# A hybrid decoder layer on one core: turning the attention probabilities with transposing DMAs, and a new slot table beside the MLP

## The chip, the cores and the metric

The kernel runs on one core of one Trainium2 chip, in one launch. The metric is the device time of that core in microseconds, lower is better. The number before the change is the median of three runs.

## The reference

One inference step of one layer for a prompt of 2048 tokens (width 1024) and 32 sampled tokens. What matters here is the banded attention (A with window 128 and sinks; C with three dilations 1, 4, 16) that is computed beside the matrix products of the layer:

```python
def hybrid_layer(h, W, l, past):
    u = rmsnorm(h, W['norm_mix_g'][l])
    proj = u @ W['w_in'][l]                      # qa ka va qc kc vc z xbc dt
...
    oa, _ = banded_attention(qa, ka, va, WIN_A, 1, tab_a, W['a_sinks'][l])
    for window, dil in C_BRANCHES:               # (128,1), (512,4), (2048,16)
        o, s = dilated_banded_attention(qc, kc, vc, window, dil, tab_c)
...
    y, h_last = ssd_chunked(xs, dt, A, bm, cm, h0)   # the scan, chunks of 128
    h = h + mixed @ W['w_out'][l]
    u2 = rmsnorm(h, W['norm_mlp_g'][l])
    h = h + jnp.square(jax.nn.relu(u2 @ W['w_up'][l])) @ W['w_down'][l]

# inside banded_attention, per block of 128 queries and its 256 keys
    logits = jnp.einsum('nbqhgd,nbshd->nbhgqs', qb, kb) + bias
    probs, lse = softmax_with_sink(logits, valid[None, :, None, None], sk)
    out = jnp.einsum('nbhgqs,nbshd->nbqhgd', probs, vb)
```

## The kernel before

The program has three parts: `tokens` and `settle` (input projection, up to about 299 us) and `core`. In `core` the 2048 + 32 tokens go in four blocks (`PIECES`, 512 tokens each, the last 512 + 32). First comes a part called the columns (`col`, to about 717 us). Then comes the trunk: for each block the output projection (`out`), its norm, and four quarters of the MLP, each eight `up` and eight `down` units. A dense unit is 24 matmuls of 128x128 by 512 columns: each product is taken three times on f16 halves (high x high, high x low, low x high).

`plan()` writes the order of all units, and every engine walks the same list. The last 16 dense units of a block host nothing, so 56 slots remain, one behind each of the others. In these slots the block b hosts the small work of block b+1, with b = 0, 1, 2 (called the first, second and third host below). The words for it are:

- a tile of attention: 128 queries by 256 keys, 4 heads. The trunk has 18 tiles in each host, 12 of them real (the others only load keys and values for their neighbour); all 36 real tiles have a previous block. `att` slot k of before does three things at once: the values of tile k-3 (`give_values`, L2573, the product with V), the turning of tile k-2 (`turn_p`, L2588: eight f32 transposes of 128x128 by TensorE into banks 3 and 4, from where ScalarE L1884 and VectorE L2142 write the high half `p_hi` and the low half `p_lo`), and the scores of tile k-1 (`score`, L2603; VectorE L2123 adds the bias and takes the top, ScalarE L1891 the exponential).
- `scan`: three parts of one chunk of the scan; part 1 keeps VectorE from L2251 to L2267. `weigh`/`turn` join the branches.
- `sk`, `sv` (L2727) with `split` (ScalarE L1975, VectorE L2385): the attention of the sampled tokens, in the second and third host.
- in the first host the weights of the MLP come raw (`core_staged`, 512 KB for a dense unit), are split by ScalarE L1794 and VectorE L2043, and are stored for the other blocks.

All DMAs of `core` are issued by SyncE (SP) in the order of the units. SP waits in order: behind a wait stand the weight loads of later units (`fetch`, four slots ahead), the loads for tiles (`load_qkv`, a transposing DMA L1450 of up to 256 KB from DRAM and a plain one L1455), and the store of a tile's output (`store_o`, L1462, waits for VectorE L2107). PSUM has two banks for dense units and six spare ones; `claim()` lets a unit wait until the last user of its bank is through.

## Time and profile before

| | us |
|---|---|
| median of 3 runs (2426.82 to 2431.17) | 2430.77 |
| the profiled execution, whole | 2431.39 |
| its span, first to last instruction | 2429.5 |
| TensorE busy | 2333.6 (96%) |
| VectorE busy | 1193.9 (49%) |
| ScalarE busy | 839.9 (35%) |
| GpSimd busy | 299.5 (12%) |
| mean TensorE clock granted | 0.988 |

TensorE is busy nearly all the time, the others half of it or less. Shares are averages: in the hosting slots VectorE, SP and the DMA engines have much more to do than in the last block. A transposing DMA stands in the trace as an instruction of SP's queue with the time that SP was held by it, and with the time from issue to landing.

### The profile page before, as it was taken

Reading aid. Unit: us, or ns where it says so; the run is one execution under the profiler, and the core shown is the slowest. Engines: PE = TensorE matmul, PEld = TensorE weight load, DVE = VectorE, ACT = ScalarE, POOL = GpSimd, SP = SyncE. Lnnn points to the kernel's source line nnn. Section 1 sums busy time; section 2 is a strip of 40 time slices with the busy share of each in tenths; the row PEclk is TensorE's granted clock in tenths of the full one; section 3 lists DMA queues with packets and bytes.
Section 4 is the critical chain, followed back from the end, with each engine's and each line's share of the span. In section 5 each row is a group of like instructions: output and inputs, shape, how many; then the busy total and the mean of one; then the engine's idle time right before and its main releaser. Section 6 shows DMA issues by size and latency. Waiting matters only on the chain. (4 is left out here: it accounts for less than half of the span.)

```text
span 2429.5 us, 42324 instructions
## 1 busy us (share of the span) xinstructions
PE 2333.6 (96%) x17134; PEld 1355.8 (56%) x17134; DVE 1193.9 (49%) x2680; ACT 839.9 (35%) x1580; POOL 299.5 (12%) x316
## 2 busy tenths in 40 slices
PE   6999889999899999999999999999999999999999
PEld 3555445555345555444555554445555456888887
DVE  5676475565647666633655562155555522321222
ACT  5454354555445445322433321034334112210110
POOL 1122223102012211001111200101111001000000
PEclk9999999999999999999999999999999999999999
DMA  7746587775558877875665565445554553222222
GB/s 253 257 165 222 177 224 197 213 223 169 174 192 224 213 212 238 260 250 158 154 159 162 167 190 171 139 132 127 151 182 157 173 159 114 89 95 96 96 96 85
DMA packets 396759, 419.94 MB, mean 173 GB/s; under 512 B 130453, under 2 KB 325525, under 8 KB 396310
## 3 DMA queue, kind: packets, MB, share of 16 engines
q1 hardware_dynamic: 396276, 416.79, 56.9%
q8 instruction: 137, 2.24, 0.4%
q14 instruction: 56, 0.46, 0.1%
q10 hardware_dynamic: 290, 0.45, 0.1%
HBM read 280.31 MB, written 118.96 MB: 164 GB/s over the span
## 5 line engine op out<-in xcount | busy, mean ns | idle before, releaser
L2478 PE MATMUL core_dense<-core_u,tok_ring 128*128 128x512 f16 (+2 forms) x4800 | 863.6, 340 | 7.8 <-DVE core_u L2063 7.5
L2478 PEld LDWEIGHTS core_dense<-core_u,tok_ring 128*128 128x128 f16 x4800 | 465.9, 98 | 377.5 <-DVE core_u L2063 11.4
L2478 PE MATMUL core_dense<-core_r_hi,tok_ring 128*128 128x512 f16 (+2 forms) x2560 | 651.4, 340 | 1.7 <-DVE core_r_lo L2082 1.7
L2478 PE MATMUL core_dense<-core_r_lo,tok_ring 128*128 128x512 f16 (+2 forms) x1280 | 434.7, 340 | 0.0
L2478 PEld LDWEIGHTS core_dense<-core_r_hi,tok_ring 128*128 128x128 f16 x2560 | 250.6, 98 | 197.5 <-DVE core_r_lo L2082 2.7
L2478 PE MATMUL core_dense<-tok_u,tok_ring 128*128 128x512 f16 x1104 | 256.0, 388 | 10.8 <-PEq L866 8.1
L1861 ACT ACTIVATE core_r<-core_dense 128x512 f32<-128x512 f32 (+2 forms) x160 | 82.3, 515 | 470.0 <-PE core_dense L2478 469.8
L2079 DVE TENSOR_TENSOR core_r<-core_r 128x512 f32<-128x512 f32 (+2 forms) x160 | 96.7, 604 | 290.0 <-ACT core_r L1861 289.6
L766 PE MATMUL tok_prod<-tok_w_hi,tok_u 128*128 128x512 f16 (+1 forms) x768 | 198.1, 347 | 3.5 <-DVE tok_u L622 3.5
L2478 PEld LDWEIGHTS core_dense<-tok_u,tok_ring 128*128 128x128 f16 x1104 | 106.8, 100 | 140.7 <-issue 19.7
L2478 PEld LDWEIGHTS core_dense<-core_r_lo,tok_ring 128*128 128x128 f16 x1280 | 125.4, 98 | 94.5 <-issue 1.5
L1891 ACT ACTIVATE core_p<-core_p,core_neg 128x256 f32<-128x256 f32 (+1 forms) x256 | 99.7, 460 | 184.6 <-DVE core_neg L2130 184.5
L2091 DVE SCALAR_TENSOR_TENSOR core_h<-core_dense,core_h 128x512 f32<-128x512 f32 (+1 forms) x96 | 58.3, 607 | 211.8 <-PE core_dense L2478 211.7
L766 PE MATMUL tok_prod<-tok_w_lo,tok_u 128*128 128x512 f16 (+1 forms) x384 | 133.2, 347 | 0.0
L2043 DVE SCALAR_TENSOR_TENSOR tok_ring<-core_staged,tok_ring 128x1024 f16<-128x1024 f32 x72 | 88.9, 1235 | 71.3 <-ACT tok_ring L1794 69.9
L1733 POOL TENSOR_TENSOR core_v_hi<-core_v_raw,core_ones 128x256 f16<-128x256 f32 (+1 forms) x82 | 62.1, 758 | 490.1 <-DMA core_v_raw<-out_tok 338.0
L766 PEld LDWEIGHTS tok_prod<-tok_w_hi,tok_u 128*128 128x128 f16 x768 | 74.6, 98 | 65.8 <-DVE tok_u L622 6.6
L2190 DVE SCALAR_TENSOR_TENSOR core_col<-core_conv_raw,core_cw,core_col 128x512 f32<-128x512 f32 x96 | 76.1, 793 | 63.0 <-ACT core_conv_raw L1815 60.8
L2082 DVE TENSOR_TENSOR core_r_lo<-core_r,core_r_hi 128x512 f16<-128x512 f32 (+2 forms) x160 | 97.2, 608 | 17.0 <-DVE core_r L2079 0.5
L2091 DVE SCALAR_TENSOR_TENSOR core_h_more<-core_dense,core_h_more 128x512 f32<-128x512 f32 (+1 forms) x64 | 36.2, 565 | 131.6 <-PE core_dense L2478 131.6
L1771 POOL TENSOR_TENSOR core_ssum<-core_ssum,core_r 128x512 f32<-128x512 f32 (+1 forms) x24 | 30.9, 1286 | 564.8 <-ACT core_r L1840 564.8
L2123 DVE CUSTOM_DVE_ANT_0 core_p<-core_spare,core_bias 128x256 f32<-128x256 f32 (+1 forms) x256 | 81.4, 373 | 23.7 <-PE core_spare L2603 18.2
(327 smaller groups left out, 2564.2 us busy)
## 6 DMA issues: line engine op xcount, KB each, us to landing
tok_ring<-scratch_kept_w SPq DMA_DIRECT2D x262, 512.0 KB, 4.4
scratch_kept_w<-tok_ring SPq DMA_DIRECT2D x72, 512.0 KB, 5.5
core_staged<-in_w_up SPq DMA_DIRECT2D x32, 512.0 KB, 4.6
core_staged<-in_w_down SPq DMA_DIRECT2D x32, 512.0 KB, 4.2
out_tok<-tok_tok SPq DMA_DIRECT2D x16, 644.0 KB, 3.1
core_piece<-in_c_kt SPq DMA_DIRECT2D x32, 288.0 KB, 3.9
core_piece<-in_c_v SPq DMA_DIRECT2D x16, 576.0 KB, 4.5
scratch_sums<-core_o SPq DMA_DIRECT2D x64, 132.0 KB, 3.6
```

What stands on the lines that cost most here:

```text
L766: last = pe.matmul(bank[0:nt, 0:w], l, r[:, k, c0:c0 + w], start=k == 0 and i == 0, stop=k == KT - 1 and i == 2, skip_group_check=True)
L1733: pool.tensor_tensor(hi, v, ones[:, 0:w].rearrange("p (h d) -> p h d", d=HD), ALU.mult).then_inc(vh_ready, 1)
L1771: pool.tensor_tensor(ssum[:, 0:w], ssum[:, 0:w], r[:, i % 2, 0:w], ALU.add).then_inc(summed, 1)
L1861: act.activation(r[:, n % 2, 0:w], bank_of["up", b, f, q][:, 0:w], ACT.Relu, scale=1.0 / (WS * HS)).then_inc(r_ready, 1)
L1891: last = act.activation(p[:, hh, cols], p[:, hh, cols], ACT.Exp, bias=neg[:, hh:hh + 1])
L2043: dve.scalar_tensor_tensor(ring[:, q % R, :, 1, :], w_raw[n % RW], WS, ring[:, q % R, :, 0, :], ALU.mult, ALU.subtract).then_inc(lo_split, 1)
L2079: dve.tensor_tensor(r2[:, n % 2, 0:w], r[:, n % 2, 0:w], r[:, n % 2, 0:w], ALU.mult).then_inc(r2_ready, 1)
L2082: dve.tensor_tensor(r_lo[:, f % HF, off:off + w], r2[:, n % 2, 0:w], r_hi[:, f % HF, off:off + w], ALU.subtract).then_inc(rl_ready, 1)
L2091: dve.scalar_tensor_tensor(here, bank_of["down", b, i, q][:, 0:w], HS * HS / WS, here, ALU.mult, ALU.add).then_inc(down_added, 1)
L2123: last = dve.tensor_tensor_reduce(p[:, hh, cols], spare[1 + bank][:, :].rearrange("p (a c) -> p a c", c=2 * P)[:, at, cols], bias[:, BIAS_ ...
L2190: dve.scalar_tensor_tensor(dst, conv_raw[:, i, j:j + 512], cw[:, i, j:j + 1], dst, ALU.mult, ALU.add).then_inc(tap, 1)
L2478: ins = pe.matmul(bank, w[:, k, part, :], s, start=first and j == 0, stop=last and j == 2, skip_group_check=True)
```

## The change

For the 36 tiles of the trunk (`by_dma`) TensorE turns nothing. ScalarE (`high`) and VectorE (`low`) write the two f16 halves of the probabilities from SBUF into `p_half`, 128 x 1024 each, and SP issues two transposing DMAs of 256 KB from SBUF to SBUF (`turn_p`, into `p_t`). The four steps of a tile are units of their own: S scores and softmax, one slot later H the halves, one slot later T the DMAs, two slots later O the values. A new tile begins every second slot. The three parts of a scan chunk now stand two slots apart in the odd slots, among the tiles, ten slots from chunk to chunk; before, they stood behind the last tile. The joins follow as before. Banks: O has bank 4, B of the scan bank 3 and CB bank 5 (chunks from 4 on), `sk` always banks 3 and 0. The bias table has two buffers in place of three, so that it is loaded again for each run of tiles of a kind. The 28 tiles before the trunk keep the old way.

```diff
-bias = a.sb("bias", [P, 3, 4, 2 * P])
+bias = a.sb("bias", [P, 2, 4, 2 * P])
...
-p_hi = a.sb("p_hi", [P, 8, P], F16)
-p_lo = a.sb("p_lo", [P, 8, P], F16)
+p_t = a.sb("p_t", [P, 2, 8, P], F16)
+p_hi, p_lo = (p_t[:, i, :, :] for i in range(2))
+p_half = a.sb("p_half", [P, 2, 8, P], F16)
+half_ready, pt_in = a.sems("half_ready", 2), a.sems("pt_in", 2)
...
+reals = [[n for n in range(first, end) if att[n][3]] for first, end in zip([0] + att_end[:-1], att_end)]
+bias_runs = [(kind, [n for n, _ in run]) for kind, run in itertools.groupby(
+    ((n, att[n][0]) for group in reals for n in group), key=lambda tile: tile[1])]
+run_of = {n: r for r, (_, run) in enumerate(bias_runs) for n in run}
+def by_dma(n):
+    return n >= att_end[1]
+def dma_no(n):
+    return real_no[n] - real_no[att_end[1]]
+HOST_FROM = (2, 2, 4)
...
-            some = [[] for _ in range(HOST_FROM[b])] + [[s] for s in att_slots(att_end[b + 1], att_end[b + 2])]
-            for c in range(4 * b + 4, 4 * b + 8):
-                x1, x2, x3 = scan_parts(c)
-                some += [[x1], [], [x2], [x3]]
+            some = [[] for _ in range(56)]
+            for m, n in enumerate(reals[b + 2]):
+                at = HOST_FROM[b] + 2 * m
+                some[at].append(("S", n, 0, 0))
+                some[at + 1].append(("H", n, 0, 0))
+                some[at + 2].append(("T", n, 0, 0))
+                some[at + 4].append(("O", n, 0, 0))
+            some[at + 6].append(("sums", 4 * b + 4, 0, 0))
+            for c in range(4):
+                for part, unit in zip((0, 2, 4), scan_parts(4 * b + 4 + c)):
+                    some[HOST_FROM[b] + 1 + 10 * c + part].append(unit)
             j = joins(b + 1)
-            some += [[j[0]], [], [j[1], j[2]], [], [j[3], j[4]], [], [j[5], j[6]], [], [j[7]]]
-            some += [[]] * (56 - len(some))
+            for k, those in enumerate(([j[0]], [j[1], j[2]], [j[3], j[4]], [j[5], j[6]], [j[7]])):
+                some[HOST_FROM[b] + 38 + 2 * k] += those
...
+SK_BANKS = (3, 0)
+def b_bank(c):
+    return 1 if c < 4 else 3
+def cb_bank(c):
+    return 2 if c < 4 else 5
+def o_bank(n):
+    return 4 if by_dma(n) else 5
...
+        def load_bias(r):
+            kind, run = bias_runs[r]
+            if r >= 2:
+                sp.wait_ge(top, real_no[bias_runs[r - 1][1][0]])
+            sp.dma_start(bias[:, r % 2, :, :], lines_at(io, kind, P - 1, [[LINE - 1, P], [P * LINE, 4], [1, 2 * P]])).then_inc(bias_in[r % 2], 16)
+        def turn_p(n):
+            e = real_no[n]
+            sp.wait_ge(o_done, e)
+            for i in range(2):
+                sp.wait_ge(half_ready[i], dma_no(n) + 1)
+                sp.dma_start_transpose(p_t[:, i, :, :], p_half[:, i, :, :].rearrange("p a c -> p (a c)")).then_inc(pt_in[i], 16)
...
+            scored = b if kind == "S" else k - 1 if kind == "att" and b <= k - 1 < i else None
+            r = run_of.get(scored, 0)
+            if r and scored == bias_runs[r][1][0] and r + 1 < len(bias_runs):
+                load_bias(r + 1)
+            if kind == "S":
+                while next_qkv < min(b + 4, len(att)):
+                    load_qkv(next_qkv)
+                    next_qkv += 1
+            elif kind == "T":
+                turn_p(b)
+            elif kind == "sums":
+                load_sums(b)
...
+        def soften(n):
+            act.wait_ge(neg_ready, real_no[n] + 1)
+            for hh in range(4):
+                last = act.activation(p[:, hh, :], p[:, hh, :], ACT.Exp, bias=neg[:, hh:hh + 1])
+            last.then_inc(p_ready, 1)
+        def high(n):
+            act.wait_ge(p_ready, real_no[n] + 1)
+            if dma_no(n):
+                act.wait_ge(pt_in[0], 16 * dma_no(n))
+            act.activation(p_half[:, 0, :, :].rearrange("p a c -> p (a c)"), p[:, :, :].rearrange("p h c -> p (h c)"), ACT.Copy).then_inc(half_ready[0], 1)
...
+        def keep_values(n):
+            e = real_no[n]
+            dve.wait_ge(o_done, e + 1)
...
+        def score(n):
+            kind, _, _, _, prev = att[n]
+            e, r = real_no[n], run_of[n]
+            cols = slice(0, 2 * P) if prev else slice(P, 2 * P)
+            if kind == 0:
+                dve.wait_ge(const_in, 64)
+            dve.wait_ge(bias_in[r % 2], 16 * (r // 2 + 1))
+            dve.wait_ge(s_done, e + 1)
...
+            if by_dma(n) and dma_no(n):
+                dve.wait_ge(half_ready[1], dma_no(n))
...
+        def low(n):
+            dve.wait_ge(half_ready[0], dma_no(n) + 1)
+            if dma_no(n):
+                dve.wait_ge(pt_in[1], 16 * dma_no(n))
+            flat = [t.rearrange("p a c -> p (a c)") for t in (p_half[:, 1, :, :], p[:, :, :], p_half[:, 0, :, :])]
+            dve.tensor_tensor(*flat, ALU.subtract).then_inc(half_ready[1], 1)
...
-            pe.wait_ge(lo_ready, 2 * e + 2)
+            if by_dma(n):
+                for i in range(2):
+                    pe.wait_ge(pt_in[i], 16 * (dma_no(n) + 1))
+            else:
+                pe.wait_ge(lo_ready, 2 * e + 2)
...
-                last = pe.transpose(spare[1][:, gr * P:(gr + 1) * P], xbc[:, c % 2, 4 + gr, :], ident[:, :])
+                last = pe.transpose(spare[b_bank(c)][:, gr * P:(gr + 1) * P], xbc[:, c % 2, 4 + gr, :], ident[:, :])
```

What stands on SP's queue in the first host, before. L1385 loads raw weights, L1392 stores split ones, L1450 and L1455 load a tile, L1462 stores an output:

```order
L1385 DMA core_staged<-in_w_up 128x8x128
L1392 DMA scratch_kept_w<-tok_ring 128x2048
L1450 DMA_TRANSPOSE core_qk_t<-scratch_tok_h 128x4x128
L1455 DMA core_v_raw<-out_tok 128x256
L1462 DMA scratch_sums<-core_o 128x264
L1385 DMA core_staged<-in_w_up 128x8x128
L1392 DMA scratch_kept_w<-tok_ring 128x2048
L1450 DMA_TRANSPOSE core_qk_t<-scratch_tok_h 128x8x128
L1455 DMA core_v_raw<-out_tok 128x256
```

And in the changed kernel, in the same host (L1417 raw weights, L1424 the store, L1502 the output, L1482 the new DMAs, L1490 and L1495 a tile):

```order
L1417 DMA core_staged<-in_w_down 128x8x128
L1424 DMA scratch_kept_w<-tok_ring 128x2048
L1417 DMA core_staged<-in_w_down 128x8x128
L1424 DMA scratch_kept_w<-tok_ring 128x2048
L1502 DMA scratch_sums<-core_o 128x264
L1482 DMA_TRANSPOSE core_p_t<-core_p_half 128x8x128 x2
L1490 DMA_TRANSPOSE core_qk_t<-scratch_tok_h 128x8x128
L1495 DMA core_v_raw<-out_tok 128x256
L1490 DMA_TRANSPOSE core_qk_t<-scratch_tok_h 128x2x128
L1495 DMA core_v_raw<-out_tok 128x128
```

The two new DMAs stand behind the store of the output of the tile before, and in front of the loads for later tiles.

TensorE in the third host, before: the scores of a tile, a dense unit, the turning of that tile, the products of a sampled piece (L2727), a dense unit.

```order
L2603 MATMUL core_spare<-core_qk_t 128x128 x24
L2478 MATMUL core_dense<-core_u,tok_ring 128x512 x24
L2588 MATMUL core_spare<-core_ident,core_p 128x128 x8
L2727 MATMUL core_spare<-core_pt,core_halves 128x16 x3
L2727 MATMUL core_spare<-core_pt,core_halves 128x8 x3
L2727 MATMUL core_spare<-core_pt,core_halves 128x2 x24
L2478 MATMUL core_dense<-core_u,tok_ring 128x512 x24
```

And changed:

```order
L2699 MATMUL core_spare<-core_qk_t 128x128 x24
L2570 MATMUL core_dense<-core_u,tok_ring 128x512 x24
L2823 MATMUL core_spare<-core_pt,core_halves 128x16 x3
L2823 MATMUL core_spare<-core_pt,core_halves 128x8 x3
L2823 MATMUL core_spare<-core_pt,core_halves 128x2 x24
L2570 MATMUL core_dense<-core_u,tok_ring 128x512 x24
```

The eight transposes between the dense unit and the sampled products are gone; nothing stands in their place.

## Rows read from the trace of the kernel before

**Rows 1.** TensorE's waits from 717 us on: total us, times, longest.

```profile
PE core_spare L2727 <- DVE core_halves L2385: 5.0, 5, 1.6
PE core_spare L2727 <- DVE core_y L2273: 2.9, 4, 1.2
PE core_dense L2478 <- DVE core_r_lo L2082: 1.7, 2, 1.2
...
PE core_spare L2727 <- DVE core_o L2107: 0.2, 1, 0.2
```

**Rows 2.** Timeline of TensorE, first host: start us, us, line, operation.

```profile
789.13 0.19 PE L2573 MATMUL core_spare<-core_v_hi,core_p_hi 128*128 128x65 f16 x1
...
789.86 1.07 PE L2588 MATMUL core_spare<-core_ident,core_p 128*128 128x128 f32 x8
790.86 0.84 PE L2603 MATMUL core_spare<-core_qk_t 64*128 64x128 f16 x24
791.64 0.39 PE L2478 MATMUL core_dense<-core_r_hi,tok_ring 128*128 128x512 f16 x1
```

**Rows 3.** L2588 in windows: PE busy (x), PEld busy (x), clock, DMA share, GB/s.

```profile
1100.00:1500.00 400.00, 12.79 (x96) 10.54 (x96) 1.00 0.58 164
```

**Rows 4.** Transposing DMAs from DRAM, 717 to 1800 us: SP held (ns), and landing.

```profile
L1450 SPq DMA_TRANSPOSE core_qk_t<-scratch_tok_h x51: 1188/1599/2477, 735.8 to 1737.2; - x51
...
DMA to landing us min/median/max: 3.8/5.6/7.3
```

**Rows 5.** DMA issues: count, KB each, median us from issue to landing.

```profile
out_y<-core_yt SPq DMA_DIRECT2D x32, 256.0 KB, 2.4
...
core_h<-scratch_xt SPq DMA_DIRECT2D x16, 256.0 KB, 4.4
```

**Rows 6.** Timeline of all engines in the third host, behind an `up` unit.

```profile
1726.34 0.19 PE L2573 MATMUL core_spare<-core_v_hi,core_p_hi 128*128 128x65 f16 x1
...
1727.16 0.84 PE L2603 MATMUL core_spare<-core_qk_t 64*128 64x128 f16 x24
...
1727.93 5.35 PE L2478 MATMUL core_dense<-core_u,tok_ring 128*128 128x512 f16 x24
...
1729.36 0.15 DVE L2107 COPY core_o<-core_spare 128x4 f32<-128x4 f32 x1
...
1730.92 0.17 DVE L2130 TENSOR_SCALAR core_neg<-core_o 128x4 f32<-128x4 f32 x1
...
1733.12 1.04 PE L2588 MATMUL core_spare<-core_ident,core_p 128*128 128x128 f32 x8
...
1733.92 1.36 DVE L2385 TENSOR_TENSOR core_halves<-core_piece,core_halves 128x1152 f16<-128x1152 f32 x1 [2.83 <-ACT core_halves L1975]
...
1735.34 0.81 PE L2727 MATMUL core_spare<-core_pt,core_halves 128*128 128x8 f16 x25 [1.18 <-DVE core_halves L2385]
```

**Rows 7.** Timeline behind a `down` unit, second host.

```profile
1246.71 0.19 PE L2573 MATMUL core_spare<-core_v_hi,core_p_hi 128*128 128x65 f16 x1
...
1247.97 0.15 DVE L2107 COPY core_o<-core_spare 128x4 f32<-128x4 f32 x1
```

**Rows 8.** Timeline of VectorE in part 1 of a scan chunk, first host.

```profile
870.85 0.68 DVE L2251 TENSOR_TENSOR core_xdt<-core_spare,core_small 128x512 f32<-128x512 f32 x1
...
872.05 0.41 DVE L2255 TENSOR_TENSOR core_cb_low<-core_spare,core_upper 128x256 f32<-128x256 f32 x1
...
877.52 0.68 DVE L2267 TENSOR_TENSOR core_state<-core_state,core_small 128x512 f32<-128x512 f32 x1
```

**Rows 9.** Timeline of TensorE in part 2 of a chunk, third host.

```profile
1788.95 0.44 PE L2708 MATMUL core_spare<-core_dec,core_xdt 128*64 128x128 f32 x4
...
1790.85 1.13 PE L2716 MATMUL core_spare<-core_xte,core_b_tok 128*128 128x256 f32 x4
```

**Rows 10.** Window, first host: PE, PEld, DVE, ACT, POOL busy (x), clock, DMA share, GB/s.

```profile
735.00:855.00 120.00, 119.42 (x1062) 66.86 (x1061) 79.06 (x201) 58.18 (x104) 24.60 (x30) 1.00 0.88 222
```

**Rows 11.** VectorE, groups from 717 to 1160 us: busy us, mean ns, idle before.

```profile
L2043 DVE SCALAR_TENSOR_TENSOR tok_ring<-core_staged,tok_ring 128x1024 f16<-128x1024 f32 x62 | 76.0, 1226 | 46.2 <-ACT tok_ring L1794 44.8
```

114 lines of the change are left out of this document (60 added, 54 removed).

## The prediction

> **What bounds the kernel.** I read the table first: TensorE is busy for 96% of the span. Then its waits from 717 us on, where the change lies: they are few, and those that the change can touch are 5.0 + 2.9 + 0.2 us before the sampled products (L2727) and 1.7 us at the start of a quarter's `down` units [rows 1]. So what leaves TensorE there leaves the time, as long as nothing new makes it wait. The timelines then show how much slack each neighbour has; "u" below is the moment at which TensorE begins a tile's values behind a dense unit, and all offsets count from it.
>
> **Part 1, the transposes leave TensorE.** In [rows 2] the eight transposes begin at 789.86 and the scores behind them at 790.86: 1.00 us for a tile. As busy time it is 12.79 us for twelve tiles, 1.07 each [rows 3]. 36 tiles: **-36 us** (ends -35 and -38). Scores, values and dense units keep their count.
>
> **Part 2, the way by DMA, and what the steps wait for.** In [rows 6] scores follow u by 0.82 (1727.16), the dense unit by 1.59 (1727.93), and it ends at +6.78 (1733.12), so it takes 5.19. In the changed order the next values stand two dense units later: 1.59 + 2 x 5.19 = **+11.97** is TensorE's own pace for a tile. The DMAs of that next tile stand on SP behind the store of this tile's output, and that waits for VectorE's copy, which ends at +3.17 behind an `up` unit (1729.51) [rows 6] and at +1.41 behind a `down` unit (1248.12 against 1246.71) [rows 7]. With some 0.35 for the store the first transposing DMA can start at +3.5 or +1.8. About half of the 36 are of each kind.
>
> How long both take is the unknown. Transposing DMAs from DRAM hold SP for 1.19 to 2.48 us, median 1.60, and land 3.8 to 7.3 after issue, median 5.6 [rows 4]; no row has one from SBUF. Two in a row: at least 1.2 + 3.8 = 5.0, at the medians 1.6 + 5.6 = 7.2, at most 2.5 + 7.3 = 9.8. Plain DMAs of 256 KB land in 2.4 us from SBUF and 4.4 from DRAM [rows 5], two us apart; I take half of that off the median: **6.2 us** for the pair. Then the values find their data at +9.7 behind `up`, +8.0 behind `down`, before +11.97, and TensorE would not wait.
>
> But there is a second loop. VectorE's `low` of a tile waits for the landing of the tile before (its buffer is single), VectorE is in order, and behind `low` stand the raw split of the first host (1.23 us) [rows 11], the `up` work (1.4) and the copy (0.5) that releases the next DMAs. Its length is 6.2 + low 1.3 + split 1.2 + up 1.4 + copy and store 0.9 = **11.0 us in the first host**, against 11.97; 9.8 in the other two. It fits by a little, until a scan chunk comes in: part 1 keeps VectorE from 870.85 to 878.20, 7.35 us [rows 8], parts 2 and 3 some 4 more with their waits on ScalarE, and TensorE gets only about 4.7 us of scan work for all three (3.0 for part 2, from 1788.95 to 1791.98) [rows 9]. Before, the chunks stood behind the tiles and this did no harm. Now three of four chunks of a host are among the tiles: +11.3 - 4.7 = 6.6 us for a chunk, less 5 tiles x 1.0 of slack in the first host, leaves some 2 us a chunk. That is 3 x 2 at the values behind the chunks, and 2 more at the first `down` units, which need the last `up` unit's low half from a late VectorE: **+8 us**. In the second host the slack of 5 x 2.2 covers the chunk; sampled products now share banks 3 and 0 with the scan, and at two slots TensorE waits some 1.5 for a copy, of which 0.9 to 1.3 each is no new kind: **+2**.
>
> The transfers: the first host already has a DMA share of 0.88 at 222 GB/s [rows 10]. 24 transfers of 256 KB are 6.3 MB more in some 175 us, 36 GB/s or 0.14 of share, about what the longer stretch for the same tiles gives back. So I add nothing, but the landing may rise here; that is in the range.
>
> **Part 3, the sampled products of the third host.** TensorE can take a piece only when VectorE has its low half. Behind `up` this is at +8.94 (1735.28) [rows 6], since the scores' softmax goes first, and TensorE came there at +7.78, after the turning of the tile: it waited 1.18. With no turning it comes at +6.78 and waits 2.2. Part of what Part 1 takes off is given back here. Over the eight pieces that stand behind a slot with scores: two beside no scan behind `up` 2.2 each, one with part 3 of the scan 1.3, one behind `down` 0.9 (there VectorE is some 1.3 earlier), together 6.6. Where part 1 of a scan stands in the slot the piece also waits for bank 5, which CB now has: L2251 to L2255 are 1.6 us [rows 8] behind `low`, so 3.3 twice, and 2.5 once behind the tiles. Part 2 of the scan has bank 5 as well, as before, but its y is now behind `low`: 2.5 and 0.8. Sum 19.0 against 8.1 before [rows 1]: **+11 us**.
>
> **Part 4, small things.** The 1.7 us at the `down` units go in their old places (their price in the new ones is in Part 2): **-1.7**. ScalarE and VectorE make the halves from SBUF instead of PSUM, 1024 columns each, no more than now. SP also passes T's waits with its weight loads behind it; those are four slots ahead, some 21 us, and SP comes free at about +10, so nothing. The bias is loaded seven times more, a run of four tiles ahead: nothing.
>
> **Sum.** 2431.4 (the profiled execution) - 36 + 8 + 2 + 11 - 1.7 = 2414.7. That execution is 0.6 above the median of the runs: **2415** after rounding up.
>
> **The rivals.** What moves the sum is the time of the DMA pair. From 6.2 to 7.4 the same walk gives 18 in the first host, 3 in the second and 14 in the third: 14 us more for 1.2 us.
>
> - *Quick landing.* The pair takes 5.0, the least that rows 4 allow: first host +3, second +1, third +8: 2431.4 - 36 + 12 - 1.7 = 2406, and 2396 if the bank waits are hidden as well. For it: SBUF as the source [rows 5]. Against it: SP was held longer in the busy first host. The Trainium skill (Advanced Engine Details and Errata, X-Bar Transpose) says that transposing DMAs on TRN2 are as fast as regular ones; rows 4 and 5 show 5.6 against 4.4 us from DRAM, so the trace does not bear it out in full, and by that rule the sum would be this rival's.
> - *Landing as from DRAM, or in a crowd.* 7.2 to 7.4 a pair: 2431.4 - 36 + 18 + 3 + 14 - 1.7 = 2429, the gain eaten; with a bit more crowding 2436.
> - *SP held per block of the source, slower than before.* If the source in SBUF makes SP issue longer, 2.5 us each, and the second lands at 7.3, the pair takes 9.8. Then the data come at +13.3 behind `up` (late by 1.4), and VectorE's loop is 14.6 in the first host and 13.4 in the others against 11.97: about 1.8 for each of 36 tiles, 66 us in place of the 10 of Part 2: 2431.4 - 36 + 66 + 14 - 1.7 = 2474. The sum passes 2431 where the pair takes some 7.6 us, and grows then by 12 or more for each us. For it: every tile pays, nothing overlaps within a pair. Against it: no row above 2.5. Where it takes 8.4, it is some 2442.
> - *Blocks one by one.* A pair has 16 blocks of 128x128. The Trainium skill (VectorE: DVE Perf Modes, The three transpose paths) gives 1309 ns for one by DMA against 390 on TensorE, and advises TensorE where PSUM will do. Eight blocks landed in 5.6 us in rows 4, not in 10.5, so the trace speaks against the sum of singles; if it held, the pair would be 21 us, the loop 27, and 36 x 14 us would make it about 2900.
>
> **How the numbers follow.** Forecast (2406 to 2424) 0.42. Quick landing, below 2406, 0.10. As from DRAM (2424 to 2437) 0.22, of which 0.03 below 2426, 0.15 within 0.2% of 2430.8 (2425.9 to 2435.6) and 0.04 above. SP held longer 0.24, blocks one by one 0.02. So faster by over 0.2% 0.55, within 0.2% 0.15, slower 0.30; 0.2% is about what a measurement of this kernel can tell from no change. The range goes from 2397 (all waits of Part 3 hidden) to 2460, which leaves out 0.03 below and about 0.14 above. The likeliest case has 2406 to 2424 of its own.
>
> **What would show it.** No L2588 row for the trunk and TensorE's busy time down by 36 to 38 us (Part 1). The new DMAs' hold and landing: a median hold of 1.6 and landing of 4.6 is the forecast; 2.5 or more is the slower rival. TensorE's waits at the values (L2573's successor) put down to the landing of `p_t` or to VectorE, some 8 to 10 us, nearly all in the first host; waits at L2727's successor near 19 us in the third host. If those at the values are above 40 us, Part 2 is wrong; if those at the sampled products are 8 us or less, Part 3 is.

## The result, and the profile after

| | median us | range | ratio to before, 95% interval |
|---|---|---|---|
| kernel before | 2428.8 | 2423.98 to 2431.17 | |
| changed kernel | 2471.6 | 2468.61 to 2473.75 | 1.0176, 1.0161 to 1.0191 |

The change makes the kernel 1.8% slower; 2415 was forecast, in a range up to 2460. The page of the changed kernel, first its table of engines: busy us, share of the span, instructions.

```profile
span 2468.0 us, 41862 instructions
...
PE 2327.9 (94%) x16846; PEld 1333.7 (54%) x16846; DVE 1191.8 (48%) x2644; ACT 836.9 (34%) x1544; POOL 306.9 (12%) x316
```

Against 2429.5 and 2333.6 before, TensorE's idle time grew from 95.9 to 140.1 us (+44.2), and its busy time fell by 5.7 us only, though 36 transposes of a tile had left it (38.1 us as busy time). To see where, cut the trace at the same four places of the program: the start of the trunk, and the last transposes of y (L2551 before, L2643 after) in each of the first three blocks. The stretches in between are the first, second and third host, and a last block that hosts nothing. Of each: start:end, length, PE busy, PEld, DVE, ACT, POOL busy, the granted clock, DMA share, GB/s. The kernel before:

```profile
717.00:1150.00 433.00, 430.18 (x2644) 218.37 (x2645) 252.30 (x487) 170.62 (x283) 57.63 (x58) 1.00 0.73 217
1150.00:1597.00 447.00, 444.71 (x3610) 229.91 (x3607) 206.59 (x493) 129.98 (x239) 52.58 (x58) 1.00 0.56 161
1597.00:2057.00 460.00, 451.64 (x3339) 251.22 (x3339) 216.54 (x527) 134.47 (x259) 48.74 (x52) 0.99 0.51 151
2057.00:2429.00 372.00, 362.51 (x3116) 304.59 (x3116) 97.90 (x212) 60.25 (x140) 0.00 (x0) 1.00 0.29 94
```

and the changed one:

```profile
715.00:1170.00 455.00, 429.31 (x2544) 211.84 (x2545) 251.50 (x474) 169.78 (x271) 57.33 (x58) 0.97 0.77 222
1170.00:1622.00 452.00, 440.14 (x3515) 222.67 (x3515) 205.72 (x482) 129.03 (x227) 56.97 (x58) 0.98 0.65 176
1622.00:2096.00 474.00, 451.58 (x3246) 244.09 (x3247) 214.91 (x515) 133.28 (x247) 51.45 (x52) 0.97 0.56 162
2096.00:2468.00 372.00, 362.23 (x3116) 304.28 (x3114) 97.40 (x211) 60.16 (x140) 0.00 (x0) 1.00 0.29 94
```

The exact lengths are 432.6, 447.4, 460.2 before and 454.9, 452.1, 473.6 after. The last block is the same to 0.1 us, so the loss is in the hosts. Length less PE busy is TensorE's idle time: 2.8, 2.3 and 8.4 us before, 25.7, 11.9 and 22.4 after. The column behind POOL is the second part of the loss: the granted clock, 1.00, 1.00 and 0.99 before, is 0.97, 0.98 and 0.97. The trace's record of the clock adds up, in the three hosts, to 3.4, 0 and 6.8 us at the half level (1.2 GHz) before, and to 27.2, 13.6 and 30.6 after (whole records; the one at the start of the first host lies over its edge, 0.7 us before and 2.3 after). Half of that time is lost. This closes the account of each host; the price paid is the measured growth plus the 12 us that the transposes had taken:

| | idle | clock | 12 tiles not turned | sum | measured | price forecast | price paid |
|---|---|---|---|---|---|---|---|
| first | +22.9 | +11.9 | -12 | +22.8 | +22.4 | +8 | 34.4 |
| second | +9.6 | +6.8 | -12 | +4.4 | +4.6 | +2 | 16.6 |
| third | +14.0 | +11.9 | -12 | +13.9 | +13.4 | +11 | 25.4 |

One number of this table leans on its execution. In the traces of two experiments below that leave the third host of the kernel before as it was, this host took 455.9 and 456.5 us, not 460.2, and had no time at the half level. Against those the third host grew by 17 us, and the account closes as well (clock +15.3). The other two are steady: 432.3 and 433.9, and 447.2.

The waits themselves, TensorE's from 717 us on (what waited and for what: us in total, times, longest), which answer to [rows 1]:

```profile
PE core_spare L2669 <- DMA core_p_t<-core_p_half: 15.1, 8, 3.7
PE core_spare L2823 <- DVE core_cb_low L2341: 9.6, 3, 3.7
PE core_spare L2823 <- DVE core_halves L2471: 8.5, 5, 2.3
PE core_spare L2818 <- DVE core_dt_all L2477: 4.7, 1, 4.7
PE core_dense L2570 <- DVE core_r_lo L2154: 4.5, 1, 4.5
PE core_spare L2812 <- DVE core_dt_all L2477: 4.4, 1, 4.4
PE core_spare L2823 <- DVE core_y L2359: 3.8, 3, 2.6
...
PE core_spare L2699 <- issue: 2.6, 1, 2.6
PE core_spare L2804 <- issue: 2.3, 2, 1.5
PE core_spare L2782 <- DVE core_dt_all L2477: 1.7, 1, 1.7
```

L2669 are the values, all eight waits in the first host; L2823 are the sampled products, L2812, L2818 and L2782 parts of the scan that wait for a bank. "issue" means that the trace shows nothing that was waited for. And how the clock looks on the way: three stretches of 20 us in the third host of the changed kernel, columns as above (before, this place had 0.92 from 1720 to 1740 and 0.99 or 1.00 beside it), and the mean time of a dense matmul between 1800 and 1822 (462 ns, against 379 to 380 at full clock):

```profile
1760.00:1780.00 20.00, 16.11 (x133) 7.98 (x132) 11.15 (x26) 10.84 (x19) 2.05 (x2) 0.91 0.70 176
1780.00:1800.00 20.00, 17.96 (x162) 9.02 (x163) 10.45 (x26) 6.46 (x11) 3.39 (x4) 0.87 0.64 170
1800.00:1820.00 20.00, 16.28 (x137) 8.58 (x135) 9.95 (x19) 7.29 (x16) 6.10 (x6) 0.84 0.83 230
```

```profile
L2570 PE MATMUL core_dense<-core_r_hi,tok_ring 128*128 128x512 f16 x36 | 13.8, 462 | 0.0
```

Last the new DMAs, the answer to [rows 4], one row for each host (SP held, ns: least, median, most):

```profile
L1482 SPq DMA_TRANSPOSE core_p_t<-core_p_half x24: 1271/2254/3651, 754.0 to 927.0; - x24
...
L1482 SPq DMA_TRANSPOSE core_p_t<-core_p_half x24: 1231/1436/3519, 1209.4 to 1372.4; - x24
...
L1482 SPq DMA_TRANSPOSE core_p_t<-core_p_half x24: 1232/1330/1722, 1659.4 to 1844.2; - x24
```

Their landing took 5.0, 4.8 and 3.2 us at the median. By these medians a pair takes 2.3 + 5.0 = 7.3 us in the first host, 6.2 in the second and 4.5 in the third; taken pair by pair, from the start of the first DMA to the landing of the second, the medians are 6.9, 6.0 and 4.8. Over all 72 the median hold is 1.47, which would hide this.

### The profile page after: what moved, and what is told of

Read it like the earlier page. It is cut to its first block, busy times and chain, and to the rows that moved or that the text cites. A ratio compares the mean times of both kernels' runs of the same rounds, so it can differ in the third digit from the quotient of the medians.

```text
span 2468.0 us, 41862 instructions
## 1 busy us (share of the span) xinstructions
PE 2327.9 (94%) x16846; PEld 1333.7 (54%) x16846; DVE 1191.8 (48%) x2644; ACT 836.9 (34%) x1544; POOL 306.9 (12%) x316
## 4 chain that ended last, share of the span: by engine, by line
PE 65%; DVE 10%; ACT 5%; DMA 3%; issue 3%; SPq 2%; POOL 0%; DVEq 0%; ACTq 0%
PE core_dense L2570 59%; DMA core_p_t<-core_p_half 2%; DVE core_col L2276 1%; PE core_spare L2669 1%; DVE core_p L2196 1%; PE core_spare L2699 1%; PE core_spare L2823 1%; ACT core_dec L2008 1%; ACT core_p L1953 1%; DVE core_p_half L2210 1%; DMA core_js<-scratch_sums 1%; SPq L1482 1%; DVE core_dec L2344 1%; DVE core_r L2151 1%; PE core_spare L2684 1%
## 5 line engine op out<-in xcount | busy, mean ns | idle before, releaser
L2570 PE MATMUL core_dense<-core_u,tok_ring 128*128 128x512 f16 (+2 forms) x4800 | 875.4, 343 | 7.8 <-DVE core_u L2135 7.5
L2570 PE MATMUL core_dense<-tok_u,tok_ring 128*128 128x512 f16 x1104 | 257.2, 390 | 11.9 <-PEq L866 8.1
L2115 DVE SCALAR_TENSOR_TENSOR tok_ring<-core_staged,tok_ring 128x1024 f16<-128x1024 f32 x72 | 90.0, 1251 | 78.1 <-ACT tok_ring L1850 76.7
L1953 ACT ACTIVATE core_p<-core_p,core_neg 128x256 f32<-128x256 f32 x144 | 61.3, 496 | 166.1 <-DVE core_neg L2203 166.1
L1784 POOL TENSOR_TENSOR core_v_hi<-core_v_raw,core_ones 128x256 f16<-128x256 f32 (+1 forms) x82 | 69.0, 842 | 359.4 <-PE core_spare L2669 207.4
L1792 POOL TENSOR_TENSOR core_grown<-core_xbc,core_grown 128x512 f32<-128x512 f32 x32 | 50.1, 1587 | 345.6 <-ACT core_grown L2005 345.6
```

Of the source, the lines that this page charges most:

```text
L1784: pool.tensor_tensor(hi, v, ones[:, 0:w].rearrange("p (h d) -> p h d", d=HD), ALU.mult).then_inc(vh_ready, 1)
L1792: last = pool.tensor_tensor(grown[:, 4 * gr:4 * gr + 4, :], xbc[:, c % 2, 6 + gr, :].unsqueeze(1).to_broadcast([P, 4, P]), grown[:, 4 * gr ...
L1953: last = act.activation(p[:, hh, :], p[:, hh, :], ACT.Exp, bias=neg[:, hh:hh + 1])
L2115: dve.scalar_tensor_tensor(ring[:, q % R, :, 1, :], w_raw[n % RW], WS, ring[:, q % R, :, 0, :], ALU.mult, ALU.subtract).then_inc(lo_split, 1)
L2570: ins = pe.matmul(bank, w[:, k, part, :], s, start=first and j == 0, stop=last and j == 2, skip_group_check=True)
```

## The experiments

Two questions: what made TensorE wait, and what a wait costs. "Hosts" are the lengths cut at the places above, in the order first, second, third, from one profiled execution; the times are medians. The kernel before took 2425.9 to 2427.3 beside these runs. The part ahead of the trunk, which no edit touches, ended between 712.9 and 720.5 us in these traces, so a difference of a few us is read from the hosts and not from the time. In short: two edits, the scan chunks put behind the tiles and one order turned round, take the changed kernel from 2471.6 to 2406.7 us.

### One part undone, one cost taken away

**Chunks behind the tiles.** Part 1, 2, 3 of chunk c at slots x, x+2, x+3, four slots from chunk to chunk, as in the kernel before:

```diff
-    some[HOST_FROM[b] + 1 + 10 * c + part].append(unit)
+    some[(29, 29, 30)[b] + 4 * c + part - part // 4].append(unit)
...
-    some[HOST_FROM[b] + 38 + 2 * k] += those
+    some[(45, 45, 46)[b] + 2 * k] += those
```

> The changed kernel, but with the scan chunks behind the tiles of each host again (parts at slots x, x+2, x+3, four slots from chunk to chunk), joins behind them; tiles, turning DMAs and banks as changed. Changed kernel 2471.6 us. Theory A (scan chunks among the tiles make VectorE late, its late halves stop TensorE at the values, and each stop is followed by a stretch at half clock): the waits for the landing of p_t (15.1 us) fall below 4, the half-clock time in the trunk (about 65 us) falls by 20 or more, and the time falls to 2440 to 2455. Rival B (the turning DMAs themselves, their landing or their traffic, cost the time wherever the scan stands): waits for p_t stay above 10 and the time within 2465 to 2475. Rival C (half clock is not tied to the waits): the time falls only by the waits taken away, some 12 us, 2458 to 2462, and the half-clock time stays near 65.

Measured 2443.9 (ratio to before 1.0069, 1.0054 to 1.0084), hosts 431.8, 438.2, 483.3. The first two fall by 23.1 and 13.9 us, the second now 9.2 shorter than before. The waits for p_t went to 8.4 us, not below 4, but with the clock (half level in the first host from 27.2 to 6.8 us) the time is in theory A's range. The third host, though, is 10 us longer. Its waits are all in one row:

```profile
PE core_spare L2823 <- DVE core_halves L2471: 28.8, 12, 4.5
```

With the chunks at the end, a scan's part and the piece for the sampled values again meet on VectorE, and the piece is behind.

**Two buffers for the halves.** `high` and `low` wait for the landing of the tile before the last.

```diff
-    p_half = a.sb("p_half", [P, 2, 8, P], F16)
+    p_halves = a.sb("p_half", [P, 2, 2, 8, P], F16)
...
-    RQ, RK, RV, RO = 3, 6, 5, 4
+    RQ, RK, RV, RO = 3, 4, 5, 4
```

> The changed kernel with two buffers for the f16 halves of the probabilities, so that VectorE and ScalarE wait for the turning DMAs of the tile before the last instead of the last (paid with four buffers for queries and keys in place of six). Changed kernel: ScalarE waits 28.6 us and VectorE 14.5 us for those landings, TensorE 15.1 us for p_t. Theory A1 (the loop through the single buffer is what carries VectorE's lateness on): ScalarE's and VectorE's waits there fall below 5 us, TensorE's for p_t below 6, time 2450 to 2460. Theory A2 (VectorE is late from its own work with a scan chunk among the tiles, the buffer only shows it): the waits for the landing go, but TensorE's stops stay, time within 2466 to 2474.

Measured 2451.0 (1.0103, 1.0086 to 1.0121); hosts 440.2, 445.4, 474.1. The waits of ScalarE and VectorE for the landing (28.6 and 14.5 us) are gone; those of TensorE for p_t are 7.6. The time is in A1's range; the waits for p_t are 1.6 above it. The second loop of the forecast is real, and it bites in the first two hosts, while the third does not move. In the second host no wait for p_t was there to lose: there one wait for VectorE's copy in front of the scan (L2818, 4.7 us) fell to 1.7, so it was `low`'s wait for the landing that had held that copy.

**No turning DMAs.**

```diff
-    sp.dma_start_transpose(p_t[:, i, :, :], p_half[:, i, :, :].rearrange("p a c -> p (a c)")).then_inc(pt_in[i], 16)
...
-    if dma_no(n):
-        act.wait_ge(pt_in[0], 16 * dma_no(n))
...
-    if dma_no(n):
-        dve.wait_ge(pt_in[1], 16 * dma_no(n))
...
-    pe.wait_ge(pt_in[i], 16 * (dma_no(n) + 1))
+    pe.wait_ge(half_ready[i], dma_no(n) + 1)
```

> The changed kernel without the 72 turning DMAs: halves are written as before, the values wait for the halves instead of the landing and read what lies in p_t (the outputs of the trunk's attention are not computed). Slot table and banks as changed. Theory A (order and banks cost most, DMAs only through their latency at the values): p_t waits (15.1 us) go nearly whole, the bank and piece waits (cb_low 9.6, halves 8.5, y 3.8, dt_all 10.8 us) stay, time 2445 to 2458, still above the kernel before at 2428.8. Rival B (the DMAs and their traffic are what costs): time below 2425, since then only the 36 us of transposes saved would remain with small waits.

Measured 2443.7 (1.0068, 1.0053 to 1.0083); hosts 432.9, 445.6, 474.2. So even with free turning the new table would lose: 16.4 us over before, though 36 us of TensorE work are gone. Some 52 us are the price of order and banks, 28 that of the DMAs, latency and traffic together. This is theory A, with a time 1.3 us under its range. The 27.7 us of the first experiment, the 20.6 of the second and these 27.9 must not be added up: all three act on the same loop, in which a late `low` waits for a landing.

**The split of the sampled values first.**

```diff
-    some[12 + 2 * k] = some[12 + 2 * k] + [("split", 16 + k, 0, 0)]
+    some[12 + 2 * k] = [("split", 16 + k, 0, 0)] + some[12 + 2 * k]
```

> The changed kernel with one order turned round: in the third host VectorE and ScalarE split the piece of the sampled values before the softmax of the scores in the same slot, not behind it. In the changed kernel TensorE waits 8.5 us in 5 stops for those low halves (sampled values, third host), and the third host takes 473.6 us against 460.2 before. Theory (the low half stands behind the softmax on VectorE, and each stop also brings a stretch at half clock): these waits fall below 1.5 us, the third host by 9 to 14 us, time 2457 to 2463 against 2471.6. Rival (the softmax is then late instead, and the wait comes back at the values or the banks): the third host changes by less than 3 us, time 2468 to 2474.

Measured 2470.4 (1.0178, 1.0159 to 1.0197), third host 474.5: nothing, as the rival said. The third host's waits before the sampled products, 21.9 us in all, became

```profile
PE core_spare L2823 <- DVE core_cb_low L2341: 14.7, 3, 6.1
PE core_spare L2823 <- DVE core_y L2359: 7.7, 3, 5.0
...
PE core_spare L2823 <- DVE core_halves L2471: 0.8, 1, 0.8
```

23.2 us: the low halves come in time, and the products now wait for bank 5, held by the scan.

**Sampled values in bank 3**, on TensorE and VectorE alike.

```diff
-    claim(("SV", b, i), 5, smp_taken, 16 + 2 * b + i + 1)
+    claim(("SV", b, i), 3, smp_taken, 16 + 2 * b + i + 1)
```

> The changed kernel with the sampled values of the third host in PSUM bank 3 in place of bank 5, which they share with CB and y of the scan. In the changed kernel TensorE waits 9.6 us in 3 stops for VectorE's copy of CB and 3.8 in 3 for y before these products. Theory (the shared bank 5 is the cause): both go below 2 us together, bank 3 is released by ScalarE and costs at most 2 us, the third host falls by 12 to 18 us with the clock, time 2453 to 2460. Rival (the sampled values stand behind VectorE's low half in those slots anyway, or bank 3 is as late): the waits only change their name, time 2466 to 2474.

Measured 2456.4 (1.0123, 1.0104 to 1.0141), third host 462.4, 11.2 us less. The waits for CB and y are gone; 4.8 us for ScalarE's `rms` in bank 3 and 1.9 more for low halves came instead. The theory holds, a little smaller.

**The store behind the turning DMAs.**

```diff
     elif kind == "O":
-        store_o(b)
+        held_back.append(b)
...
+    if held_back and kind != "T":
+        store_o(held_back.pop())
```

> The changed kernel with the store of a tile's output issued behind the turning DMAs of the next tile instead of ahead of them, so that these no longer wait for VectorE's copy of the values. Theory (the walk of the forecast: the store's wait for the copy, 1.4 to 3.2 us behind the values, is in the loop of every tile): the turning DMAs start that much earlier, TensorE's waits for p_t fall from 15.1 us to below 6, the first host from 455.0 to 443 or less, time 2457 to 2463 against 2471.6. Rival (VectorE's low half comes last at the DMAs, so the store hides behind it): waits and time stay, 2467 to 2473.

Measured 2462.2 (1.0146, 1.0125 to 1.0166), hosts 451.2, 450.0, 473.9; waits for p_t 11.7. The time is within the theory's range, the waits and the first host (443 or less was expected) lie between the two expectations: the store's wait is in the loop, but only a few us of it come last.

### What a wait costs

**Twelve pauses in the last block** of the kernel before, where nothing is hosted.

```diff
+    if unit[0] in ("up", "down") and unit[1] == NB - 1 and unit[2] % HF >= 2 and unit[2] < 3 * HF and unit[2] % 4 == 3 % 4:
+        units.append(("pause", 0, 0, 0))
...
+    pool.wait_ge(up_done if up else down_done, ...)
+    pool.tensor_tensor(zs[:, 0, :, :], ...)
+    pool.tensor_tensor(m[:, :, :], ...).then_inc(paused, 1)
...
+    pe.wait_ge(paused, pauses)
```

> The kernel before, with 12 pauses put into TensorE in the last block, which hosts nothing: behind every fourth dense unit of its first three quarters TensorE waits for two GpSimd operations (1.27 us each) that begin when the unit has ended, about 2.8 us a pause, 33 us in all. It measures the price of a wait. Theory A (a wait costs its length and a stretch at half clock behind it): 1.2 us or more for each pause beyond its length, the time rises by 45 us or more over 2428.8, and the granted clock of the last block, 1.0 now, falls to about 0.9. Rival C (a wait costs its length): the time rises by 31 to 36 us and the clock stays at 0.98 or more there.

Measured 2464.7 (1.0158, 1.0142 to 1.0173), and the last block went from 372.3 to 410.1 us, +37.8:

```profile
PE core_dense L2491 <- POOL core_m L1782: 27.4, 12, 2.4
```

27.4 us are the waits; the clock record has 17.0 us at the half level in this block, 8.5 lost. Together 35.9, so 1.9 stay open. Neither expectation hit: a pause of 2.3 us costs 3.1. The pauses lie some 25 us apart, and the clock fell to its half level five times.

**The same in the second host**: `unit[1] == 1` in place of `NB - 1`, and three operations of 224 columns.

> The kernel before with 12 pauses of TensorE in the second host (behind every fourth dense unit of the first three quarters it waits for three GpSimd operations that begin when the unit has ended, some 2.5 to 3 us). In the last block, beside no other work, 12 waits of 2.3 us (27.4 us) cost 37.4 us. Theory A (a wait costs more beside the hosted work, since scores, values, turning and scan have TensorE less filled): half clock for 20 us or more in the second host, 1.0 us or more per pause on top of its length. Rival (it is the same everywhere): 0.5 to 0.9 us per pause on top.

Measured 2470.0 (1.018, 1.0164 to 1.0195). The second host went from 447.4 to 489.9, +42.5:

```profile
PE core_dense L2495 <- POOL core_idle L1784: 10.3, 4, 3.2
PE core_spare L2590 <- POOL core_idle L1784: 8.5, 3, 3.8
PE core_spare L2744 <- POOL core_idle L1784: 8.5, 4, 2.5
...
PE core_spare L2620 <- POOL core_idle L1784: 2.8, 1, 2.8
```

30.1 us of waits and 23.9 us at the half level, 12.0 lost: 42.1. A wait of 2.5 us costs 3.5 here, 1.0 on top of its length, so the theory holds by a hair. In the changed kernel the hosts' idle time grew by 46.5 us and the clock took 30.6 more, an even larger share (0.66 us for each us of wait, against 0.40 here and 0.31 in the last block). This is the term that the forecast did not have.

### Putting it together

**All four changes**: chunks behind, two buffers, split first, store behind.

> Turning by DMA with four changes to the changed kernel: scan chunks behind the tiles, two buffers for the halves (four for queries and keys), the split of the sampled values ahead of the softmax, and the output's store behind the next turning DMAs. With the chunks behind the tiles alone it was 2443.9 us: first host 431.8, second 438.2, third 483.3 (before 432.6, 447.4, 460.2), with 8.4 us of waits for p_t and 28.8 us for the low halves of the sampled values. Theory (waits and the clock behind them ate the 36 us that the transposes give): both waits below 4 us, first host 424 or less, third host 448 to 455, time 2402 to 2414, faster than the kernel before (2427 to 2429). Rival (the turning DMAs have a price of their own that no order takes away): time 2420 or more.

Measured 2406.1 (0.9918, 0.9899 to 0.9938), faster than before by 0.8%. Its three hosts, columns as above:

```profile
715.00:1147.00 432.00, 423.51 (x2547) 209.07 (x2548) 250.85 (x475) 169.87 (x272) 56.14 (x58) 0.99 0.82 234
1147.00:1585.00 438.00, 434.23 (x3514) 219.62 (x3512) 202.98 (x481) 128.85 (x227) 56.99 (x58) 1.00 0.70 182
1585.00:2027.00 442.00, 436.56 (x3244) 240.72 (x3243) 214.30 (x516) 134.00 (x247) 54.47 (x52) 1.00 0.64 174
```

The exact hosts are 431.3, 438.8, 441.7, so -1.3, -8.6, -18.6 (-14.5 against the two shorter third hosts above). Part 1 promised 12 each: the third has it, the second most of it, the first nearly nothing. The time is in the theory's range; the first host (424 or less) and the waits for p_t (5.2 us, not below 4) are not.

**The same split in the kernel before**, the diff of "split first" there.

> The kernel before (TensorE turns) with one order turned round: in the third host VectorE and ScalarE split the piece of the sampled values before the work of the tiles in the same slot. The version with turning DMAs that has this and three more changes took 2406.1 us against 2426.6 before; this run tells how much of that any kernel would get from the split's place. Theory (before waits 4.7 us there in 5 stops and has 6.8 us at half clock in the third host, and no more is to be had): third host 460.2 falls by 4 to 9 us, time 2418 to 2424. Rival (the split's place was the whole gain, the DMAs bring nothing): time 2406 to 2410.

Measured 2425.2 (0.9999, 0.9989 to 1.001): no difference. The third host has 454.8, 5.5 less than in the trace before, but only 1 to 2 less than in the two other traces of it. With TensorE turning, the 5.0 us of waits for low halves [rows 1] only change place:

```profile
PE core_spare L2588 <- ACT core_p L1891: 5.1, 4, 1.5
```

The transposes need the softmax in the same slot. With turning by DMA nothing on TensorE does, so the piece can go first for free. This is a gain of the DMAs that the forecast did not see.

**The table kept**, chunks among the tiles, all else repaired (two buffers, split first, bank 3, store behind).

> The changed kernel with its table kept (scan chunks among the tiles) and the other waits taken out: two buffers for the halves (four for queries and keys), the split of the sampled values first, these in bank 3, the output's store behind the next turning DMAs. With the chunks behind the tiles the like took 2406.1. Theory (a chunk among the tiles costs by itself, since VectorE has no room for it there): TensorE still waits 10 us or more for low halves, p_t or copies in the first host, time 2420 to 2440. Rival (the chunks' place only mattered through the single buffer and bank 5): time 2402 to 2412.

Measured 2430.7 (1.0015, 1.0006 to 1.0024), hosts 442.7, 447.8, 447.6. 24.6 us slower than with the chunks behind the tiles (11.4, 9.0 and 5.9 by host), within the theory's range: with all else repaired the chunks' place still costs all that was won. The two versions differ in one more thing, bank 3 in place of 5, so the third host is not clean: its longest waits are 5.7 us for ScalarE's `rms` in bank 3. The waits that stay elsewhere are 4.6 us for `r_lo`, 8.9 for p_t in the first host, and 4.4 + 1.7 + 1.7 for banks in the second.

**One buffer again**, in the version with 2406.1.

> The fastest version so far (2406.1 us: chunks behind the tiles, two buffers for the halves, the split first, the store behind) with the single buffer for the halves again and six buffers for queries and keys. Theory (the second loop, VectorE's low half waiting for the landing, bites only where something makes VectorE late, and the chunks were that): time 2404 to 2412. Rival (the loop is at its limit in the first host by itself): waits for p_t rise from 5.2 to over 10 us and the time to 2415 or more.

Measured 2406.5 (0.9921, 0.9904 to 0.9938): in the time the buffer is worth nothing once the chunks are out of the way. It was worth 20.6 us with them in. In the traces the first host is 435.3 against 431.3 and TensorE waits 8.7 us for p_t against 5.2, so up to 4 us may hide in the scatter.

**Two changes only**, chunks behind and split first.

> The changed kernel with two changes only: scan chunks behind the tiles and the split of the sampled values first. With two more (store behind, two buffers) it was 2406.1, with the store behind 2406.5. Chunks behind alone 2443.9, split first alone 2470.4. Theory (the two causes were the chunks for the first and second host, the split for the third once the chunks are gone; the store's place adds only the few us of p_t waits in the first host): time 2407 to 2415. Rival (the store ahead of the turning DMAs holds every tile of the first host): time 2416 or more.

Measured 2406.7 (0.9917, 0.9901 to 0.9934). These two are all that is needed. Alone they gave 27.7 and 1.2 us, together 64.9. So with the split first in both, the chunks' place is worth 63.7 us (2470.4 against 2406.7); by host 19.5, 12.6 and 32.7.

**No turning DMAs in this order**: the version with 2406.5 and the diff of "no turning DMAs" above.

> Chunks behind the tiles, split first, store behind, single buffer, as the version with 2406.5 us, but without the 72 turning DMAs and without the waits for them (the outputs of the trunk's attention are not computed). That version: first host 435.3, second 439.9, third 442.4 us; before 432.6, 447.4, 460.2. Theory (the landing of p_t and its traffic hold the first host, where the raw weights also come in): first host 420 to 425, second and third within 2 us of 439.9 and 442.4, time 2392 to 2400. Rival (the first host is held by VectorE and ScalarE in this order, not by the DMAs): first host 430 or more, time 2402 or more.

Measured 2389.0 (0.9846, 0.9831 to 0.986); hosts 419.4, 439.9, 439.3. In the first host:

```profile
714.00:1134.00 420.00, 419.17 (x2548) 208.52 (x2549) 250.66 (x476) 168.89 (x272) 58.07 (x58) 1.00 0.75 226
```

TensorE is idle for 0.8 us and the host is 13.2 shorter than before, Part 1 to the full. With the DMAs it is 435.3: here they cost the whole gain, 15.9 us (14.5 against the version with two changes, 11.9 against the one with two buffers); in the second host they cost nothing, in the third 3.1. The theory holds, with a time 3 us under its range. Against the changed kernel without its turning DMAs (2443.7), order alone is worth 54.7 us. In the version with 2406.5 a turning DMA of this host holds SP for 2.7 us at the median:

```profile
L1482 SPq DMA_TRANSPOSE core_p_t<-core_p_half x24: 1990/2736/4263, 752.1 to 902.4; - x24
...
DMA to landing us min/median/max: 5.8/7.2/8.8
```

The landings of this trace are those of the first DMA of each pair alone, since records of the other semaphore are missing. The version with two changes has all 24: SP held 2.57, landing 5.7 at the median. Both are longer than the changed kernel's 2.25 and 5.0; the DMA share of this host is 0.83 there, against 0.77. TensorE waits again, mostly here, at values and scores (8.7 and 4.5 us in the trunk); for the scores the trace names no releaser.

**Other banks behind the tiles** in the version with 2406.1: once the tiles are through.

```diff
-    SK_BANKS = (3, 0)
+    def sk_banks(n, j):
+        return (3, 0) if 2 * n + j < 9 else (1, 4)
+    def sv_bank(n, j):
+        return 5 if 2 * n + j < 9 else 4
```

> The version with 2406.1 us, with other banks behind the tiles, where scores and values no longer use theirs: sampled keys in banks 1 and 4 instead of 3 and 0, sampled values in bank 4 instead of 5. It waited there 2.1 + 1.2 + 1.3 us for VectorE's copies. Theory (these waits go, with no half clock behind them since none fell there): 3 to 5 us less, 2401 to 2403. Rival (they stand beside waits that end as late): 2405 to 2407.

Measured 2400.4 (0.9893, 0.9878 to 0.9908), the fastest version, 1.1% under the kernel before. Hosts 431.8, 435.4, 442.0: the second is 3.4 shorter than without, for 3.1 us less of idle time, as the theory said, and it is now the full 12.0 shorter than before. The rest of the 5.7 us between the two medians is in no host.

## Why the prediction was wrong

**The step that failed** is the price of a scan chunk among the tiles, in Part 2: some 2 us of wait a chunk in the first host, nothing in the second. With the chunks behind the tiles these hosts are 23.1 and 13.9 us shorter. The second error is a term that was put at nothing without a reason: every wait was priced at its length alone. In numbers, the forecast had 19 us of new waits and no clock (8 + 2 + 11 - 1.7); idle time in the hosts grew by 46.5, and the clock took 30.6 more. That is 58 us above the forecast, and the miss is 57.

**Part 1** was right in its size, 1.0 us a tile. Without the turning DMAs, in the last order, TensorE's busy time is 2297.0, 36.6 less than before, and the hosts are 13.2, 7.5 and 20.9 us shorter. The first is what 12 tiles give. The second lacks 4.5, of which 1.5 more of idle time and 3.4 us more at the half level make 3.2; in the version with other banks it is 12.0 shorter. The third has lost 5.2 us of idle time and 6.8 at the half level besides. In the changed kernel the busy time shows little of it (-5.7 for -36 to -38), since matmuls at the half level last longer.

**Part 2** failed, in three steps.
- *The pair of 6.2 us* was right over all, and wrong where it counted: 7.3 in the first host (6.9 pair by pair). The forecast took one number for three hosts, though it had read a DMA share of 0.88 in the first [rows 10], and its own walk gave +18 there for 7.4. [rows 4] mix the hosts, too. Host by host the trace before had shown it, in the first and the second:

```profile
L1450 SPq DMA_TRANSPOSE core_qk_t<-scratch_tok_h x18: 1608/2024/2277, 735.8 to 850.9; - x18
...
L1450 SPq DMA_TRANSPOSE core_qk_t<-scratch_tok_h x18: 1189/1232/2477, 1168.5 to 1290.1; - x18
```

- *The chunk among the tiles* was the main error. The slack was summed over five tiles as if VectorE could draw on it in any order; but it is in order, and each queue ahead of a low half counts on its own. (This is read from the stops; no run has a chunk among the tiles with more room around it.) The waits for p_t became 15.1 us where 6 were forecast. The longest stop of the first host is at the first `down` unit, 4.5 us at 777.28 for `r_lo`, where this part had 2:

```profile
764.81 0.63 ACT L2015 ACTIVATE core_m<-core_y 128x512 f32<-128x512 f32 x1 [4.04 <-POOL core_y L1813]
...
771.91 1.70 ACT L1953 ACTIVATE core_p<-core_p,core_neg 128x256 f32<-128x256 f32 x4 [4.38 <-DVE core_neg L2203]
...
774.60 1.23 DVE L2115 SCALAR_TENSOR_TENSOR tok_ring<-core_staged,tok_ring 128x1024 f16<-128x1024 f32 x1 [2.72 <-ACT tok_ring L1850]
...
777.28 0.39 PE L2570 MATMUL core_dense<-core_r_hi,tok_ring 128*128 128x512 f16 x1 [4.46 <-DVE core_r_lo L2154]
```

  Read it from the end: `r_lo` was late because VectorE's raw split (L2115) had to come first and had nothing to work on for 2.7 us; ScalarE makes the raw weights' high half only after the softmax (L1953), and that was late because ScalarE had waited 4.0 us for the scan's y (L2015), and VectorE behind it. With the chunks behind the tiles this stop is gone, in the first experiment and in all later versions.
- *The second host* at +2: the step "TensorE waits some 1.5 for a copy" had 4.4, 4.7 and 1.7. The copies of the sampled keys stand on VectorE behind softmax and `up` work, and 3 us of the 4.7 behind `low`'s wait for a landing (they go with the second buffer). In the trace of the changed kernel, the copy and who waited:

```profile
1213.79 0.16 DVE L2477 COPY core_dt_all<-core_spare 128x12 f32<-128x12 f32 x1
...
1214.09 1.61 PE L2812 MATMUL core_spare<-core_xte,core_b_tok 128*128 128x256 f32 x4 [4.38 <-DVE core_dt_all L2477]
```

The mark that the prediction set for Part 2, 40 us at the values, was set wrong as well: they show 15.1, and the part failed by waits elsewhere.

**Part 3** was right: 19.0 us of waits forecast, 21.9 found (CB 9.6, halves 8.5, y 3.8), each for the reason given. Its price was 25.4, by the clock. What it did not see is that these waits, too, hang on the chunks' place: with the chunks behind and the split first they are gone, and the third host is 441.8.

**The missing term.** All parts priced a wait at its length. The two runs with pauses give 0.9 and 1.0 us more for each wait of some 2.4 us, 0.7 and 1.0 of it by the clock. Of the 76 us paid in the hosts, 30.6 are clock. The forecast's own 21 us of new waits would have brought 8 to 14 us more at the shares of 0.40 to 0.66 above, 2423 to 2429 in place of 2415: no gain to speak of. The rest is the sizes of Part 2.

**Part 4**: the 1.7 us at the `down` units became 4.5 at the first of them, where Part 2 had given them 2; the bias reloads cost nothing that the trace shows.

**The rivals.** "Blocks one by one" (2900) was far off. "As from DRAM" came nearest in mechanism for the first host, but had no time above 2436. "SP held" had 2474, and that it is close to 2471.6 is luck: it let every tile pay 1.8 us for a pair of 9.8, but SP was held for 1.47 us at the median, and TensorE waited for p_t eight times in 36 tiles, all in the first host. No rival had the clock.

What stays open: 1.9 us of the pauses in the last block; how the 28 us that the DMAs cost in the changed table divide between latency and traffic; and what the new banks for O, B and CB cost by themselves, which no run puts back alone (the sampled values' bank is worth 15.2 us of time in the changed kernel).

## What to carry to other kernels

Before spreading work among other work, follow the in-order engine that serves both, and price each queue that a needed result comes to stand behind; slack does not add up over slots. Price a new wait of a nearly full TensorE at its length and the clock behind it, here a third to two thirds more, read from the clock column of rows like it. Read the time of a DMA in the stretch where it will run, not over the whole trace. When an operation leaves an engine, look which orders it had forced there: here the piece's split could go first for nothing only without it, and to leave it behind cost 37 us (2443.9 against 2406.7), as much as the operation had taken. Fixes of one order need not add up: alone the two edits gave 27.7 and 1.2 us, together 64.9.

## What was not expected of the hardware

- Short waits of a nearly full TensorE bring the granted clock to its half level again and again: twelve waits of 2.2 to 2.4 us, some 25 us apart, gave 17.0 us of it, twelve of 2.0 to 3.8 us in the second host 23.9. The changed kernel, with waits of 1 to 5 us, has 71.4 us in its three hosts, against 10.2 before.
- A transposing DMA of 256 KB from SBUF to SBUF holds SP for 1.33 us at the median in the host where the DMA share is 0.56, and 2.25 where it is 0.77; landing 3.2 and 5.0 us. From DRAM, up to 256 KB, it had been 1.60 and 5.6 over all [rows 4]. That is not the source's doing alone: in the changed kernel the same loads from DRAM (L1490) hold SP for 1.28 us at the median and land in 3.6, in all three hosts alike.
